# Five products of constants by PE in front of each expert of layer two but the first

## The chip, the cores and the metric

The kernel runs on one core of a Trainium2 chip. Its engines are PE (matrix multiplication, with its weight loads shown apart as PEld), DVE, ACT, POOL and SP; SP only issues transfers here. The metric is the time of the kernel on the device in microseconds; the kernel before was timed three times.

## The reference, cut to what matters

The model has two layers on 256 latent and 256 context tokens of width 1024. Each layer has a mixer (two attentions and a convolution) and then a mixture of experts. The change touches the experts of layer two, where only the 256 latent tokens are left and each goes to two of 16 experts:

```
def grouped_moe(h, router_w, router_bias, w1, w3, w2):
    s = jax.nn.sigmoid((h @ router_w).astype(jnp.float32))
    ...
    _, idx = lax.top_k(jnp.where(in_grp, biased, -jnp.inf), TOP_K)
    ...
    for e in range(N_EXPERTS):
        he = (jax.nn.silu(h @ w1[e]) * (h @ w3[e])) @ w2[e]
        out = out + combine[:, e:e + 1] * he
    return out
```

w1 and w3 of an expert are 1024 x 512 and w2 is 512 x 1024, all fp32, so each of the three is 2 MB, and an expert's weights are 6 MB. After the last layer a normalisation gives the output.

## The kernel before, in words

**Steps.** The rows that go to one expert are gathered and padded to blocks of 32. One block is one step: PE makes the product with w1 and w3 in 64 multiplications of 256 columns (bank 2, "W13" below), ACT makes a sigmoid, DVE multiplies (line 1877) and transposes (line 1881), and PE makes the product with w2 in 32 multiplications (bank 3). PE runs the product with w2 of the step before behind the W13 product of this one, so a step of PE is 96 multiplications; POOL scatters the result rows.

**Experts.** The function `expert` (from line 2318) is the part of one expert. It reads the expert's number of blocks from memory into a register (line 2333), runs the first step, and, if there are more blocks, a loop of further steps (from line 2338). Expert 0 to 3 are written out, 4 to 15 are a loop of four turns over three experts. Before its first multiplication `step` (from line 2294) waits for the previous step's hidden rows (line 643, `hold`), for the transposed rows of this one, and for the landing of w1 and w3.

**Weights.** SP issues the loads in the order w1, w3, w2 of each expert, into three groups of three places of 2 MB (the places are ring, HT and parts of area; once XG). Before each load SP waits until the load before the last one has landed, so about two loads are under way, and until PE has freed the place. The list `free` hands two semaphores to the first two multiplications of the next expert: they free the places of w1 and w3 of the expert before. The place of w2 is freed by the drain at line 2315, behind the first step of the next expert.

**The end.** After the last product with w2 (of expert 15) come its scatter, the sum of the two rows of each token, the last normalisation and the stores.

Of the kernel before, what the change touches and what calls it, by code (L numbers as in the profile page):

```python
# [16 lines left out]
DEPTH = 2  # L17
# [22 lines left out]
CHUNK = 512  # L40
# [314 lines left out]
def hybrid_moe_kernel(nc, A):  # L355
# [4 lines left out]
    with ctx:  # L360
        def sb(name, shape, dt=fp32):
            return ctx.enter_context(nc.sbuf_tensor(name, shape, dt))
# [13 lines left out]
        cst = sb("cst", [P, C_W])  # L376
# [144 lines left out]

        ps = ctx.enter_context(nc.psum_tensor("ps", [P, 8, CHUNK], fp32))

        B_W13, B_W2 = 2, 3


        modD = nc.dram_tensor("mod_rows", [DEPTH, 2, 6 * D], fp32).ap()
# [112 lines left out]
        def hold(e, semaphore, value, passed):  # L640

            e.wait_ge(semaphore, value)
            e.sem_inc(passed, 1)
# [5 lines left out]
        ident = cst[:, C_ID:C_ID + P]  # L649
# [16 lines left out]
        def unit_of_slot(x):  # L666

            return ring[:, x] if x < RING else extra[x - RING].rearrange("p (k n) -> p k n", k=KD)

        def is_spare(l, e, turn, w):  # L670

            return isinstance(turn, int) and (e, w) == (GROUPS, 0)

        def spare_of(l):

            if l == DEPTH - 1:
                return [XG[:, 2:TILES + 2].rearrange("p t d -> p (t d)").rearrange("p (k n) -> p k n", k=KD)]
            return [piece.rearrange("p (k n) -> p k n", k=KD // 2) for piece in (gate.rearrange("p c d -> p (c d)"), area[:, AW - UNIT // 2:AW])]
# [22 lines left out]
        def expert_slots(l, e):  # L701

            return EXPERTS[l][0][e % GROUPS]
# [9 lines left out]
        def landed(l, e, x, turn=0):  # L713

            return 16 * pieces(x) * (expert_uses(l, e, x, turn) + 1)
# [1203 lines left out]
        def _(pe):  # L1919
            t_ = nc.tensor  # L1920

            def mm(out, lhsT, rhs, first, last_):
                return t_.matmul(out, lhsT, rhs, start=first, stop=last_)  # L1923
# [91 lines left out]
            for l in range(DEPTH):  # L2015
# [277 lines left out]
                def step(slots, prev_slot, waits, free=(), first=False, up=None, release=None):  # L2293
                    b = pe.snap(done)
                    if not first:
                        hold(pe, g_rdy[l], b, pe_passed)
                    pe.wait_ge(xt_rdy[l], b + 1)
                    if waits:
                        for q in range(2):
                            pe.wait_ge(ring_full[slots[q]], waits[q])  # L2300
                    half = NG // 2
                    up = up or [[unit_of_slot(x)] for x in slots[:2]]
                    for k in range(KD):
                        lhsT = xT[:, k * SLOT:(k + 1) * SLOT]
                        for j in range(NG):
                            last = mm(ps[SLOT * j:SLOT * (j + 1), B_W13, 0:NW], lhsT,
                                      up[j // half][k * len(up[j // half]) // KD][:, k % (KD // len(up[j // half])), j % half * NW:(j % half + 1) * NW],
                                      k == 0, k == KD - 1)
                            if k * NG + j < len(free):
                                last.then_inc(ring_free[free[k * NG + j]], 1)  # L2310
                    last.then_inc(w13_full[l], 1)
                    if not first:
                        w2_product(b, prev_slot, waits[2] if waits else None)
                        if release is not None:
                            pe.drain().then_inc(ring_free[release], 1)
                    pe.reg_add(done, done, 1)

                def expert(e, turn, at_e, first=False):

                    sl, before = expert_slots(l, e), expert_slots(l, e - 1)  # L2320
                    waits = [landed(l, e, x, turn) for x in sl[:2]]
                    free, release = [], None
                    if not first:
                        waits.append(landed(l, e - 1, before[2], turn))

                        free = [before[0], before[1]]
                        if l == DEPTH - 1 or isinstance(turn, int) and e < GROUPS:
                            release = before[2]
                        elif not isinstance(turn, int):
                            free.append(expert_slots(l, e - 2)[2])  # L2330
                    else:
                        waits.append(None)
                    blocks = pe.value_load(nb[0:1, bass.ds(at_e, 1)], min_val=1, max_val=TOK // SLOT)
                    up = [spare_of(l) if is_spare(l, e, turn, w) else [unit_of_slot(sl[w])] for w in range(2)]
                    if l == 0 and is_spare(l, e, turn, 0):
                        pe.wait_ge(spare_in, 16)
                    step(sl, before[2], waits, free, first, up, release)
                    with pe.If(blocks > 1):

                        hold(pe, ring_full[sl[2]], landed(l, e, sl[2], turn), pe_passed)  # L2340
                        with pe.Fori(1, blocks):
                            step(sl, sl[2], None, up=up)

                expert(0, 0, 0, True)
                for e in range(1, GROUPS + 1):
                    expert(e, 0, e)
                with pe.Fori(1, (E_N - 1) // GROUPS) as i:
                    for q in range(GROUPS):
                        expert(1 + q, i, 3 * i + 1 + q)
# [32 lines left out]
```

## Time and profile before

| | us |
|---|---|
| median of three runs | 1142.3 (1140.0 to 1145.42) |
| the profiled execution, time | 1148.53 |
| the profiled execution, span of the trace | 1146.7 |
| PE busy in the span | 924.9 (81%) |
| DMA into ring from the expert weights, issue to landing, median | 10.2 |
| mean granted clock of PE | 0.9 |

The profile is of one execution. Its time holds 1.83 us that lie around the span. A granted clock of 1.00 is 2.4 GHz, of 0.50 is 1.2 GHz; a value between is a mean over a stretch that has both. PE's busy time counts a multiplication until its modelled end, so neighbours overlap.

### The profile page before, as it was taken

How to read it: one execution, taken by the hardware profiler on the slowest of the kernel's cores; microseconds unless marked ns; L12 is line 12 of the kernel's file. 1: busy time of each engine (PE TensorE's matmuls, PEld its weight loads, DVE VectorE, ACT ScalarE, POOL GpSimd, SP SyncE). 2: the span in 40 equal slices, each digit the busy share in tenths (PEclk: the TensorE clock that was granted, in tenths of full speed). 3: DMA queues.
4: the chain of work that ended last, by engine and by line, in shares of the span. 5: the costliest groups of instructions: out<-in, count | busy, mean ns of one | idle time of the engine just before them, and what ended most of it. 6: DMA issues, size and time to landing. Idle time of an engine off the chain costs nothing. (4 is left out here: it accounts for less than half of the span.)

```text
span 1146.7 us, 23528 instructions
## 1 busy us (share of the span) xinstructions
PE 924.9 (81%) x8592; PEld 545.5 (48%) x8593; DVE 448.7 (39%) x1049; ACT 248.4 (22%) x491; POOL 227.0 (20%) x375
## 2 busy tenths in 40 slices
PE   3999999988897599979779399999896577555871
PEld 3546446455454356646446166544653344322440
DVE  2187515654554323323222566426633322111223
ACT  2100111543321122313122030124421112111110
POOL 4100000110020144425333220001000133211231
PEclk9999999989988699989899699999897689877886
DMA  9998601820004989999999977128206899999993
GB/s 348 380 413 299 245 3 71 339 93 1 1 19 159 374 316 405 422 416 417 422 420 411 388 288 283 74 74 340 110 1 225 323 413 398 417 428 426 417 379 117
DMA packets 54014, 317.45 MB, mean 277 GB/s; under 512 B 7288, under 2 KB 8008, under 8 KB 35136
## 3 DMA queue, kind: packets, MB, share of 16 engines
q1 hardware_dynamic: 41168, 286.21, 62.1%
q0 software_dynamic: 9584, 20.02, 4.9%
q10 hardware_dynamic: 3200, 10.36, 2.4%
q8 instruction: 43, 0.70, 0.2%
q14 instruction: 19, 0.16, 0.0%
HBM read 308.62 MB, written 12.65 MB: 280 GB/s over the span
## 5 line engine op out<-in xcount | busy, mean ns | idle before, releaser
L1923 PE MATMUL ps<-ring,area 128*32 128x256 f32 x3808 | 243.5, 407 | 63.6 <-DMA ring<-in_w 38.5
L1923 PE MATMUL ps<-ring,HT 128*128 128x512 f32 (+1 forms) x576 | 259.1, 603 | 2.3 <-ACT HT L1164 1.5
L1923 PE MATMUL ps<-area 128*32 128x256 f32 (+3 forms) x1928 | 225.3, 399 | 20.9 <-DVE area L1821 9.7
L1923 PEld LDWEIGHTS ps<-ring,area 128*32 128x32 f32 x3808 | 142.1, 117 | 154.3 <-issue 49.8
L1923 PEld LDWEIGHTS ps<-ring,HT 128*128 128x128 f32 x576 | 110.4, 197 | 128.7 <-issue 126.5
L1923 PEld LDWEIGHTS ps<-area 128*32 128x32 f32 (+2 forms) x1928 | 129.7, 139 | 45.4 <-issue 25.3
L1923 PE MATMUL ps<-HT,area 128*32 128x256 f32 x704 | 93.9, 426 | 40.9 <-DMA area<-in_w 32.3
L971 POOL DMA_INDIRECT expert_rows<-area x64 | 69.0, 1079 | 248.9 <-DVE area L1871 111.2
L1844 DVE STREAM_TRANSPOSE area<-area 128x256 f32<-128x256 f32 x65 | 29.0, 446 | 226.0 <-PE ps L1923 225.7
L1217 ACT ACTIVATE area<-ps 128x128 f32<-128x128 f32 x63 | 17.5, 278 | 362.7 <-PE ps L1923 362.7
L961 POOL DMA_INDIRECT area<-h_rows,area x68 | 71.3, 1048 | 100.4 <-DVEq L1834 42.4
L1217 ACT ACT_TABLE_LOAD x63 | 80.8, 1283 | 38.7 <-issue 37.6
L1923 PEld LDWEIGHTS ps<-HT,area 128*32 128x32 f32 x704 | 51.6, 122 | 76.1 <-issue 59.1
L1923 PE MATMUL ps<-HT,ring 128*128 128x256 f32 (+1 forms) x320 | 85.0, 423 | 1.9 <-DVE HT L1403 1.8
L1439 DVE SCALAR_TENSOR_TENSOR area<-area,CW 128x512 f32<-128x512 f32 (+1 forms) x120 | 68.8, 614 | 4.5 <-issue 0.5
L1923 PEld LDWEIGHTS ps<-HT,ring 128*128 128x128 f32 x320 | 60.1, 191 | 21.6 <-issue 15.3
L855 POOL TENSOR_SCALAR ms<-ss 128x1 f32<-128x1 f32 (+1 forms) x22 | 9.4, 428 | 237.1 <-DVE ss L1608 162.6
L1923 PE MATMUL ps<-ring,SC 128*32 128x512 f32 (+1 forms) x576 | 48.2, 489 | 9.3 <-POOLq L992 8.3
L876 POOL DMA_DIRECT2D area<-in_b_ada x20 | 10.2, 515 | 222.7 <-ACTq L637 96.4
L1156 ACT ACTIVATE area<-ps 128x512 f32<-128x512 f32 (+1 forms) x48 | 25.2, 526 | 101.6 <-PE ps L2203 68.0
L1570 DVE TENSOR_REDUCE mx<-ps 128x2 f32<-128x1024 f32 (+1 forms) x36 | 37.6, 1045 | 16.1 <-PE ps L1923 15.8
L1869 DVE COPY area<-ps 128x256 f32 (+1 forms) x39 | 16.6, 425 | 62.6 <-PE ps L1923 59.3
(221 smaller groups left out, 734.5 us busy)
## 6 DMA issues: line engine op xcount, KB each, us to landing
ring<-in_w SPq DMA_DIRECT2D x64, 2048.0 KB, 10.2
ring<-in_w_ada SPq DMA_DIRECT2D x24, 2048.0 KB, 18.7
area<-in_w SPq DMA_DIRECT2D x21, 1024.0 KB, 11.2
ring<-in_w_in SPq DMA_DIRECT2D x10, 2048.0 KB, 16.3
HT<-in_w SPq DMA_DIRECT2D x10, 2048.0 KB
area<-in_w SPq DMA_DIRECT2D x10, 2048.0 KB, 10.5
ring<-in_w_out SPq DMA_DIRECT2D x4, 2048.0 KB, 8.4
area<-expert_rows ACTq DMA_DIRECT2D x12, 512.0 KB, 5.2
```

The source lines that it names most:

```text
L855: link(g.tensor_scalar(m_, s_, 1.0 / n, EPS, ALU.mult, ALU.add))
L876: pool.dma_start(bias_of(n)[32 * j:32 * j + 32, :], A["b_ada"][l_:l_ + 1, col:col + CHUNK].broadcast_to([32, CHUNK])).then_inc(bias_in[n % ...
L961: pool.indirect_dma_start(xg[:, r * NW:(r + 1) * NW], None, h2_rows, bass.IndirectOffsetOnAxis(ap=at_, axis=0), bounds_check=routed(l) * N ...
L971: pool.indirect_dma_start(y_rows, bass.IndirectOffsetOnAxis(ap=sidx[r], axis=0), ym[:, r * NW:(r + 1) * NW], None, bounds_check=2 * routed ...
L1156: taken(s.activation(aT[:, k % 2, 0:kw], bank(key)[:, 0:kw], ACT.Identity), key)
L1217: s.activation(sg, ps[:, B_W13, 0:P], ACT.Silu).then_inc(si_rdy[l], 1)
L1439: v.scalar_tensor_tensor(dst, src, w, dst, ALU.mult, ALU.add)
L1570: v.tensor_reduce(mx[:, b], pair[:, :, 0:kw], AX.X, ALU.max)
L1844: v.transpose(xT, xs).then_inc(xt_rdy[l], 1)
L1869: v.tensor_copy(dst, ps[:, B_W2, 0:NW]).then_inc(y_rdy[l], 1)
L1923: return t_.matmul(out, lhsT, rhs, start=first, stop=last_)
```

## The change

The expert part of layer two gets five multiplications of the identity matrix with the first 512 columns of the constants, into bank 5 of ps, which nothing reads. They stand behind the load of the count and ahead of every wait of the step, in each expert but the first: 15 experts, 75 multiplications. They wait for nothing and set no semaphore.

```diff
-        B_W13, B_W2 = 2, 3
+        B_W13, B_W2, B_IDLE = 2, 3, 5
...
                     blocks = pe.value_load(nb[0:1, bass.ds(at_e, 1)], min_val=1, max_val=TOK // SLOT)
+                    if l == DEPTH - 1 and not first:
+                        for _ in range(5):
+                            mm(ps[:, B_IDLE], ident, cst[:, 0:CHUNK], True, True)
```

First place: PE, layer two, from the end of expert 0's part to the first multiplications of expert 1, before. TENSOR_LOAD is the load of the count; hidden_made, xT_copied and ring_full are the waits for the hidden rows, for the transposed rows and for the landed weights.

```order
L2316 ISA
L2341 COMPARE_AND_BRANCH
L2338 UNCONDITIONAL_BRANCH
L2333 TENSOR_LOAD area
L2333 ISA x2
L2297 REGISTER_ALU [waits hidden_made_1]
L1923 MATMUL ps<-ring,area 32x256 [waits ring_full_3,ring_full_2,xT_copied_1]
L1923 MATMUL ps<-ring,area 32x256 x31
L1923 MATMUL ps<-ring,area 32x256 [waits ring_full_1,y_copied_1,gT_copied_1]
```

The same place now:

```order
L2316 ISA
L2344 COMPARE_AND_BRANCH
L2341 UNCONDITIONAL_BRANCH
L2333 TENSOR_LOAD area
L2333 ISA x2
L1923 MATMUL ps<-cst 128x512 x5
L2297 REGISTER_ALU [waits hidden_made_1]
L1923 MATMUL ps<-ring,area 32x256 [waits ring_full_3,ring_full_2,xT_copied_1]
L1923 MATMUL ps<-ring,area 32x256 x31
L1923 MATMUL ps<-ring,area 32x256 [waits ring_full_1,y_copied_1,gT_copied_1]
```

The five multiplications have come in between the load of the count and the three waits. Everything behind them stands as it did.

Second place: PE, the third expert of the loop's body, which is expert 6, 9, 12 and 15, before:

```order
L2316 ISA
L2341 COMPARE_AND_BRANCH
L2338 UNCONDITIONAL_BRANCH
L2333 ISA
L2333 TENSOR_LOAD area
L2333 ISA x2
L2297 REGISTER_ALU [waits hidden_made_1]
L2300 ISA [waits ring_full_5,xT_copied_1]
L1923 MATMUL ps<-ring,area 32x256 [waits ring_full_0]
L1923 MATMUL ps<-ring,area 32x256 x31
```

And now:

```order
L2316 ISA
L2344 COMPARE_AND_BRANCH
L2341 UNCONDITIONAL_BRANCH
L2333 ISA
L2333 TENSOR_LOAD area
L2333 ISA x2
L1923 MATMUL ps<-cst 128x512 x5
L2297 REGISTER_ALU [waits hidden_made_1]
L2300 ISA [waits ring_full_5,xT_copied_1]
L1923 MATMUL ps<-ring,area 32x256 [waits ring_full_0]
L1923 MATMUL ps<-ring,area 32x256 x31
```

Here too the five stand behind the load and ahead of the waits. The steps inside the `If` (a second and third block) have none in front.

## Rows read from the trace of the kernel before

**Rows 1.** Busy time by engine in stretches of layer two's experts.
```profile
core 0: us, PE busy (x) PEld busy (x) DVE busy (x) ACT busy (x) POOL busy (x), PEclk, DMA share, GB/s
911.00:914.00 3.00, 1.74 (x35) 1.14 (x33) 1.16 (x4) 1.56 (x2) 0.26 (x2) 1.00 0.14 52
914.00:920.00 6.00, 3.86 (x72) 2.51 (x64) 1.59 (x5) 1.56 (x2) 1.80 (x3) 1.00 0.99 362
1000.00:1060.00 60.00, 31.70 (x384) 16.64 (x384) 7.18 (x20) 6.24 (x8) 9.32 (x16) 0.73 1.01 425
1085.00:1112.00 27.00, 21.52 (x384) 13.48 (x384) 8.22 (x23) 6.25 (x8) 11.34 (x18) 0.99 1.01 420
1112.00:1119.00 7.00, 6.55 (x68) 3.12 (x72) 0.00 (x0) 0.00 (x0) 0.12 (x1) 0.55 0.47 198
```

**Rows 2.** SP's own waits, 905 to 925: total us, times, longest.
```profile
SPq L643 <- PE ps L1923: 8.7, 2, 7.9
SPq L643 <- PEq L2315: 4.3, 1, 4.3
```

**Rows 3.** The same, 925 to 1110.
```profile
SPq L643 <- DMA ring<-in_w: 102.2, 23, 5.7
```

**Rows 4.** Timeline of PE: start, length, what, [idle before <- releaser].
```profile
905.15 6.07 PE L1923 MATMUL ps<-ring,area 128*32 128x256 f32 x64 [7.24 <-DVE area L1844]
912.48 5.39 PE L1923 MATMUL ps<-ring,area 128*32 128x256 f32 x96 [1.26 <-DVE area L1877]
922.13 0.64 PE L1923 MATMUL ps<-HT,area 128*32 128x256 f32 x2 [4.27 <-issue]
...
955.45 0.41 PE L1923 MATMUL ps<-HT,area 128*32 128x256 f32 x2 [1.88 <-DMA area<-in_w]
```

**Rows 5.** Timeline of PE, experts six and seven.
```profile
971.94 5.12 PE L1923 MATMUL ps<-ring,area 128*32 128x256 f32 x64 [2.54 <-DMA ring<-in_w]
...
987.79 7.07 PE L1923 MATMUL ps<-ring,area 128*32 128x256 f32 x96 [2.62 <-DMA ring<-in_w]
```

**Rows 6.** Timeline of PE, experts twelve to fifteen.
```profile
1064.56 6.57 PE L1923 MATMUL ps<-ring,area 128*32 128x256 f32 x64 [8.02 <-DMA ring<-in_w]
...
1073.90 10.57 PE L1923 MATMUL ps<-ring,area 128*32 128x256 f32 x192 [1.04 <-issue]
1084.97 5.39 PE L1923 MATMUL ps<-ring,area 128*32 128x256 f32 x96 [0.50 <-issue]
...
1106.56 2.11 PE L1923 MATMUL ps<-area 128*32 128x256 f32 x34
1112.45 6.52 PE L1923 MATMUL ps<-ring,area 128*32 128x256 f32 x64 [3.78 <-DMA ring<-in_w]
1118.80 1.90 PE L1923 MATMUL ps<-area 128*32 128x256 f32 x32
1122.45 1.93 PE L1923 MATMUL ps<-ring,area 128*32 128x256 f32 x32 [1.75 <-DVE area L1881]
```

**Rows 7.** Timeline of SP's DMA issues.
```profile
913.21 0.33 SPq L811 DMA_DIRECT2D ring<-in_w  x1
918.03 0.33 SPq L813 DMA_DIRECT2D ring<-in_w  x1
923.46 5.04 SPq L811 DMA_DIRECT2D ring<-in_w  x2
```

**Rows 8.** Timeline of PE, projections of layer two.
```profile
740.04 13.90 PE L1923 MATMUL ps<-ring,HT 128*128 128x512 f32 x32
```

**Rows 9.** Multiplications into ps: duration in ns, min/median/max, first and last start.
```profile
L1923 PE MATMUL ps<-ring,HT x576: 379/592/1201, 70.2 to 876.5; 128*128 128x512 f32 x181, 128*128 128x256 f32 x11
```

**Rows 10.** Line 2333, the count's load, 917 to 923: ns, start.
```profile
L2333 PEldq TENSOR_LOAD <-area x1: 301/301/301, 921.0 to 921.0; - x1
```

**Rows 11.** The same, 1060 to 1110.
```profile
L2333 PEldq TENSOR_LOAD <-area x3: 297/302/306, 1083.7 to 1107.5; - x3
```

**Rows 12.** Line 2338, the branch behind a step, 917 to 923: ns, start.
```profile
L2338 PEldq COMPARE_BRANCH  x1: 2812/2812/2812, 918.2 to 918.2; - x1
```

## The prediction

> **What bounds the kernel now.** I read the busy table by stretches first. In the experts of layer two the DMA share is 0.99 to 1.01 from 914 to 1112 at 362 to 425 GB/s, while PE is busy 31.70 of 60 us in 1000 to 1060 [rows 1]: the weights set the pace. SP's own waits say the same for 925 to 1110: 102.2 us in 23 waits end with a landing in ring [rows 3], and the view lists no wait for PE in that stretch. Two parts are different, and the change is judged in them.
>
> At the start, 905 to 925, SP waits for PE: 8.7 us in two waits, and 4.3 us for the drain at line 2315 [rows 2]. Between 911 and 914 the DMA share is 0.14 [rows 1], since the load of expert 3 that SP issues at 913.21 [rows 7] needs a place that the first multiplications of expert 1, at 912.48 [rows 4], set free. What comes late here is late for every load behind it.
>
> At the end PE is the bound. Expert 12 starts at 1064.56 when its weights have landed, and then the three loads of the count in 1060 to 1110, from 1083.7 to 1107.5 [rows 11], are those of experts 13, 14 and 15. So expert 12 has three steps: 64 and 32 multiplications from 1064.56, and 192 from 1073.90 that end at 1084.47. From there to 1106.56 + 2.11 = 1108.67 PE never waits for a landing: a 0.50 us gap at 1084.97, and others of about a microsecond between steps. Then it waits 3.78 us, to 1112.45, for w3 of expert 15 [rows 6]. All that follows hangs on that W13 product: the chain goes over it, the w2 product at 1118.80 and the last one at 1122.45 to the end.
>
> **The price of five products.** 32 multiplications of 128x512 by 128x128 weights take 13.90 us with the clock at its upper level, 0.434 each [rows 8], weight loads hidden. Five are 2.17 us. At the lower level I take twice that, 4.34; the longest single record of the form, 1201 ns against a median of 592 [rows 9], agrees with a factor of two. They wait for nothing, so they run at once behind the load of the count, which PE's sequencer reads ahead of the array (1107.5 for expert 15 [rows 11], while the array works until 1108.67). They fill the beginning of a wait and leave its end idle.
>
> Here a rule of the Trainium skill would raise the price: "FP8 and Floating Point Precision", section TensorE Precision Notes, has true fp32 as four passes through the array. By it 512 columns would be 2048 cycles at 2.4 GHz, 0.85 us, and five 4.3. The row does not bear that out: 0.434 us is 1042 cycles, two to a column. By the page the sum would be that of the doubled cost below, about 1151; I go by the row.
>
> **Part one: experts 1 and 2, where DMA waits for PE.** Expert 0's W13 product runs from 905.15 to 911.22, then PE waits 1.26 us for the hidden rows [rows 4]. The products put 2.17 in the place of 1.26: expert 1 starts 0.91 later, SP's issue at 913.21 too, and the gap of the DMA queue widens by that. Queued behind them on PE is the whole of expert 1, so the drain comes 0.91 later and with it the issue at 918.03 [rows 7].
>
> In front of expert 2 PE is idle 4.27 us [rows 4], of which 2.81 are the branch behind expert 1's step [rows 12]; the count's load follows at 921.0 [rows 10]. So the products can only start where W13 starts now, some 922.1 + 0.9 = 923.0. PE has then been idle over 4 us, and a wait of 2.5 or 2.6 us elsewhere has already brought the lower clock: 64 multiplications in 5.12, and 96 in 7.07 against 5.39 [rows 5, 6]. I take the lower level, 4.34: W13 of expert 2 starts at 927.4 instead of 922.13, and the load that SP issues at 923.46, which its first multiplications set free, goes out at about 928.7. That is no loss as long as the load ahead keeps the queue busy. It went out at 918.03 and now at 918.9; SP's next issue after 923.46 comes 4.7 us later, when it has landed (the row holds two issues, 0.33 each, in 5.04 us [rows 7], so the second went out at 928.17). With the shift it has landed by 929.1, and the new load's first bytes come about a microsecond after its issue (the share climbs at 914 after the issue at 913.21 [rows 1, 7]), at 929.7. I add 0.8 for this gap (between 0, if the clock stays up, and 5.3, if nothing of it is hidden). Together the stream of weights is 0.91 + 0.8 = 1.7 us later.
>
> **Part two: experts 3 to 12, beside the DMA.** Experts 3, 4 and 5 add 2.17 each to a PE that had 1.88 us to spare at expert 5 [rows 4]. It falls some 9 us behind the weights, and that matters only if a place is then freed too late. Three groups of places give three experts' lead: the place that expert e frees is for expert e + 2 or later, whose load goes out some 10 us or more later. The tightest is HT for expert 5, freed by expert 3; I find 1 to 2 us to spare there with the delays above and cost it at nothing; with less cover it is the rival below. Experts 6 and 7 waited 2.54 and 2.62 us [rows 5], and from 1000 to 1060 PE is idle for 28.3 of 60 us [rows 1]: PE has caught up soon after expert 7, and what it gains or loses up to expert 12 is cover. Expert 12 starts with the landing, so 1.7 later than now. Its wait, 8.02 less 2.17, is still 5.8 us, so its W13 stays at the lower clock as now (6.57).
>
> **Part three: experts 13, 14 and 15, where PE is the bound.** At expert 13 the products take up the gap of 0.50: 2.17 - 0.4 = 1.8 on the path. At expert 14, where no gap is left, 2.17. At expert 15 2.17. So without the shift the W13 product of expert 15 could start at 1108.67 + 1.8 + 2.17 + 2.17 = 1114.8, against 1112.45 now: 6.1 us of products, 3.78 of them in the wait, 2.4 on the path. In return PE has no wait left and the clock does not fall. Now 64 multiplications take 6.52 [rows 6], and 96 at the upper clock 5.39, so 64 are 3.59: 2.9 less. The product ends at 1118.4 instead of 1119.0, that is 0.5 earlier. The load of w3 also lands 1.7 later, at 1114.1 in place of 1112.45, as PE does, and PE remains the later one.
>
> **The sum.** +1.7 from part one, +2.4 and -2.9 from part three: +1.2 us. The profiled execution's 1148.53 would become 1149.7. It was 6.2 above the median of 1142.3, so I put the same difference on the median: 1143.5 us. The runs differ by 5.4 us among themselves, and a measurement of this kernel can tell about 0.5%, 5.7 us, from no change: what I forecast is no change.
>
> **Rivals.** *The clock stays up everywhere.* If the products in the waits also keep the upper clock through expert 12's wait, its W13 gives 6.57 - 3.59 = 3.0 back. PE could then start expert 15 at 1114.8 + 1.7 - 3.0 = 1113.5, and the landing at 1114.1 becomes the bound: W13 ends at 1117.7, 1.3 earlier than now, and the time is 1141.0. For it: PE's gaps shrink in 15 places, and at 955.45 a wait of 1.88 did not bring the lower clock [rows 4]. Against: the products stand at the start of the wait and 5.8 us stay empty. The Trainium skill has this as a rule ("TensorE: Matmul & The Clock Gate", section Why this matters for your kernels: no long idle gaps between bursts if the clock is to stay up); rows 5 agree as to short gaps, and by the rule this rival is right only where the rest of the gap is short.
>
> *Late places stop the weights.* This one ends slower. If nothing hides the 5.3 us of expert 2's products and expert 3's 2.17 also hold the load into HT, the stream is 0.9 + 5.3 + 2.2 = 8.4 later, and with -0.5 at the end it is +7.9: 1150.2. It decides once SP's issue of expert 4's first load is more than about 5 us later than now while the DMA share in the 5 us behind it drops under 0.9. For it: SP did wait for PE here [rows 2]. Against: two loads are under way, and each is about 5 us of transfer.
>
> *The products cost as much as at the lower clock everywhere.* Then 4.34 instead of 2.17 falls on experts 13 to 15, 6.5 more, and 1 to 2 more at the start: 1151 or so. Only a clock that does not rise, or a weight load that is not hidden, could do it; the stretch 1085 to 1112 has a clock of 0.99 [rows 1].
>
> *The products do nothing.* Were they absent from the trace, the time would be 1142.3. The order of PE's instructions has them in six places, three written out and three in a loop of four turns.
>
> **Chances.** The forecast 0.60, the clock rival 0.17, late places 0.12, the doubled cost 0.05, the rest 0.06 for things not seen here, of either sign. Slower by over 0.5% (over 1148.0) takes the late places, the doubled cost and a little of the rest: 0.14. Faster by over 0.5% (under 1136.6) is in none of the cases worked out; I leave 0.06. Within 0.5%: 0.80. The range is from 1138.5, the clock rival less half the spread of the runs, to 1150, just short of late places in full.
>
> **What would show it.** In the profile after: 75 multiplications from the constants of 128x512, a group of five in some 2.2 us; those of expert 2 in about 4.3 us. SP's issue at 913.2 about 0.9 later, expert 12's start 1 to 3 us later. The W13 product of expert 15 with no wait for a landing in front and in some 3.6 us, its start 2 to 4 us later. PEclk 1.00 between 1085 and the end of that product. It is wrong if expert 12 starts over 4 us later (part one or two), if expert 12's W13 takes under 5 us (the clock rival), or if five products take over 3 us in experts 13 to 15.

## The result, and the profile after

| | before | after |
|---|---|---|
| median of the timed runs, us | 1143.37 (1140.0 to 1145.42, 5 runs) | 1154.38 (1151.09 to 1158.46, 5 runs) |
| the profiled execution, time and span | 1148.53, 1146.7 | 1151.09, 1149.3 |
| mean granted clock of PE | 0.900 | 0.933 |
| MATMUL records in the trace | 8592 | 8742 |

The ratio of the runs is 1.0078, with a 95% interval of 1.0054 to 1.0103: the change costs 8.9 us (6.2 to 11.8). I had forecast +1.2, no change that can be told.

The profiled execution of before, 1148.53, took longer than each of its five timed ones, that of after is the shortest of its five. What differs between them ahead of the change is seen in one number: expert 0's first product starts at 905.15 before and at 898.93 after. So I compare from that start on. It leaves 1146.7 - 905.15 = 241.6 us before and 1149.3 - 898.93 = 250.4 after, +8.8, which is what the timed runs say. All times "after expert 0's start" below are made in this way. One trace is one execution; how far such numbers differ from one execution to the next is measured at the end of the experiments.

The first thing to see is the count. 75 products were added in the code, and 8742 - 8592 = 150 records. This is the view by tile for the constants, PE, in the experts of layer two; the columns are count, duration in ns (min/median/max), first and last start:

```profile
L1923 PE MATMUL ps<-cst x150: 592/592/1061, 904.7 to 1117.6; 128*128 128x512 f32 x150
```

The timeline of PE after (start, length, what, idle before and who ended it), which answers to [rows 4 to 6]:

```profile
898.93 5.80 PE L1923 MATMUL ps<-ring,area 128*32 128x256 f32 x64 [7.60 <-DVE area L1844]
...
909.14 5.39 PE L1923 MATMUL ps<-ring,area 128*32 128x256 f32 x96
916.60 6.25 PE L1923 MATMUL ps<-cst 128*128 128x512 f32 x10 [2.07 <-issue]
```

```profile
1049.20 0.41 PE L1923 MATMUL ps<-HT,area 128*32 128x256 f32 x2 [3.92 <-DMA area<-in_w]
...
1057.56 4.55 PE L1923 MATMUL ps<-cst 128*128 128x512 f32 x10 [1.29 <-issue]
1064.27 3.66 PE L1923 MATMUL ps<-ring,area 128*32 128x256 f32 x64 [2.16 <-DMA ring<-in_w]
...
1081.15 4.56 PE L1923 MATMUL ps<-cst 128*128 128x512 f32 x10
1085.64 5.39 PE L1923 MATMUL ps<-ring,area 128*32 128x256 f32 x96
...
1113.61 4.56 PE L1923 MATMUL ps<-cst 128*128 128x512 f32 x10
1118.10 3.66 PE L1923 MATMUL ps<-ring,area 128*32 128x256 f32 x64
```

Each group of five products is ten records and holds PE for 4.49 us (1081.15 to 1085.64, start to start), not the 2.17 of the forecast. From expert 0 on PE waits for no landing until expert 11, at 1049.20; before, the first such wait was that of expert 5, at 955.45 [rows 4]. Behind expert 12 there is no wait at all: the W13 product of expert 15 starts when its products end and runs at the upper clock, 3.66 us. It starts 1118.10 - 898.93 = 219.2 us after expert 0, against 207.3 before.

SP's issues after, to set beside [rows 7], and its waits for PE in 898 to 925 and in 925 to 1110 [rows 2, 3]:

```profile
909.91 0.33 SPq L811 DMA_DIRECT2D ring<-in_w  x1
...
923.69 2.57 SPq L811 DMA_DIRECT2D ring<-in_w  x2
...
939.85 0.33 SPq L811 DMA_DIRECT2D HT<-in_w  x1
```

The issue into HT before, which [rows 7] does not show:

```profile
938.60 0.33 SPq L811 DMA_DIRECT2D HT<-in_w  x1
```

The waits after:

```profile
SPq L643 <- PE ps L1923: 15.6, 2, 10.8
```

```profile
SPq L643 <- DMA ring<-in_w: 102.1, 23, 6.1
...
SPq L643 <- PE ps L1923: 3.4, 2, 1.8
```

Its waits for PE have grown from 8.7 to 15.6 us, and in the second stretch there are now two, 3.4 us, where the view had none. After expert 0's start, the first issue, the one behind expert 2's products and the one into HT come at 11.0, 24.8 and 40.9 us, against 8.1, 18.3 and 33.4.

The stretches that answer to [rows 1] (the same columns):

```profile
905.00:909.00 4.00, 4.00 (x10) 1.52 (x8) 1.07 (x4) 1.36 (x2) 1.41 (x3) 1.00 0.08 27
...
1000.00:1060.00 60.00, 49.13 (x527) 25.15 (x527) 8.98 (x25) 7.80 (x10) 13.59 (x22) 0.97 1.01 424
...
1112.00:1119.00 7.00, 7.00 (x61) 3.17 (x56) 1.79 (x5) 1.56 (x2) 2.03 (x4) 1.00 0.49 200
```

In 905 to 909 the queue stands nearly empty (0.08) while PE makes products; from 1000 to 1060 PE is busy 49 of 60 us instead of 31.7 at the same DMA share; in 1112 to 1119 the clock is 1.00, where it was 0.55.

### The profile page after: what moved, and what is told of

The parts are those of the page before. It is cut to its first block and busy times, and to the rows that moved or that the text cites. A ratio compares the mean times of both kernels' runs of the same rounds, so it can differ in the third digit from the quotient of the medians.

```text
span 1149.3 us, 23828 instructions
## 1 busy us (share of the span) xinstructions
PE 965.3 (84%) x8742; PEld 558.4 (49%) x8743; DVE 448.9 (39%) x1049; ACT 248.3 (22%) x491; POOL 226.4 (20%) x375
## 5 line engine op out<-in xcount | busy, mean ns | idle before, releaser
L1923 PE MATMUL ps<-ring,HT 128*128 128x512 f32 (+1 forms) x576 | 255.8, 597 | 2.5 <-ACT HT L1164 1.2
L1923 PE MATMUL ps<-ring,area 128*32 128x256 f32 x3808 | 228.8, 389 | 32.2 <-DVE area L1844 13.1
L1923 PE MATMUL ps<-area 128*32 128x256 f32 (+3 forms) x1928 | 216.4, 389 | 19.4 <-DVE area L1821 9.7
L1923 PEld LDWEIGHTS ps<-ring,area 128*32 128x32 f32 x3808 | 134.1, 113 | 119.0 <-issue 27.8
L1923 PEld LDWEIGHTS ps<-area 128*32 128x32 f32 (+2 forms) x1928 | 126.5, 135 | 42.5 <-issue 23.3
L1923 PE MATMUL ps<-HT,area 128*32 128x256 f32 x704 | 87.8, 406 | 23.2 <-DMA area<-in_w 18.9
L1923 PE MATMUL ps<-cst 128*128 128x512 f32 (+1 forms) x182 | 75.7, 560 | 11.6 <-issue 11.6
L1923 PEld LDWEIGHTS ps<-HT,area 128*32 128x32 f32 x704 | 48.7, 117 | 57.6 <-issue 37.0
L1923 PEld LDWEIGHTS ps<-cst 128*128 128x128 f32 x182 | 32.0, 193 | 54.1 <-issue 54.1
L855 POOL TENSOR_SCALAR ms<-ss 128x1 f32<-128x1 f32 (+1 forms) x22 | 9.4, 426 | 230.6 <-DVE ss L1608 159.4
```

What stands on the lines that cost most here:

```text
L855: link(g.tensor_scalar(m_, s_, 1.0 / n, EPS, ALU.mult, ALU.add))
```

## The experiments

The theory after the first result, T: a product of fp32 is two records, five of 512 columns are 4.5 us, and they cost where PE is on the path. That is in two places: the first experts, where they hold back SP's loads, and experts 13 to 15. The rival, R: the products disturb transfers or code fetch, so that the cost goes with the amount of added work wherever it stands. All kernels are the changed one with these lines edited; each was timed on one chip with the kernel before, except where the text says that there is one trace alone.

**Half the columns.**

```diff
-                            mm(ps[:, B_IDLE], ident, cst[:, 0:CHUNK], True, True)
+                            mm(ps[:, B_IDLE, 0:CHUNK // 2], ident, cst[:, 0:CHUNK // 2], True, True)
```

> Five products in front of the same 15 experts, but of 256 columns instead of 512. Theory (each product is two MATMUL records of 0.45 us at 512 columns, so five are 4.5 us, and they cost where PE is on the path: experts 1 and 2, then 13 to 15): five are now 2.2 us, the size that the prediction had assumed, and its own working should hold: stream of weights +1.7 us, products on the path at the end +2.4, clock -2.9, so +1.2 us, within 0 to +4. Rival (products disturb the weight transfers or PE's instruction fetch, so the cost goes with the amount of added work, wherever it stands): half of the change's +8.9, +4.5 us.

Ratio 1.0009 (0.9988 to 1.0030): +1.0 us (-1.4 to +3.4). R's +4.5 (half of +8.9) is outside. From expert 0's start to the end it is 1145.2 - 903.43 = 241.8 us, +0.2. PE's timeline:

```profile
909.56 2.42 PE L1923 MATMUL ps<-cst 128*128 128x256 f32 x10
911.92 5.39 PE L1923 MATMUL ps<-ring,area 128*32 128x256 f32 x96
```

```profile
1064.23 6.01 PE L1923 MATMUL ps<-ring,area 128*32 128x256 f32 x64 [4.93 <-DMA ring<-in_w]
...
1111.69 2.43 PE L1923 MATMUL ps<-cst 128*128 128x256 f32 x10
1114.05 3.66 PE L1923 MATMUL ps<-ring,area 128*32 128x256 f32 x64
```

A group is 2.36 us from start to start (909.56 to 911.92), the size that I had given to five full products, and with it the sum of the prediction, +1.2, comes out. Expert 12 starts at 160.8 us, and expert 15's product, with no wait before it, ends at 1114.05 + 3.66 - 903.43 = 214.3 us, against 213.8 before. So the weights are 1.4 us later at expert 12, and the stretch from there to the end of expert 15's product is 53.5 us for 54.4, 0.9 shorter; the forecast had +1.7 and -0.5.

**The first three alone.**

```diff
-                    if l == DEPTH - 1 and not first:
+                    if l == DEPTH - 1 and not first and isinstance(turn, int):
```

> Five products of 512 columns in front of experts 1, 2 and 3 alone. Theory: these are the ones that hold SP's loads; the weights come 5 to 6.5 us later for all of the layer, and the end is as in the kernel before, with its wait of 3.8 us and its lower clock: +5 to +6.5 us. Expert 12's first product starts about 165 us after expert 0's instead of 159.4. Rival (cost by amount of work, 3 of 15 places): +1.8 us.

Ratio 1.0032 (1.0012 to 1.0053): +3.7 us (1.4 to 6.1). Less than I expected in the middle, and its interval holds both; the trace tells more:

```profile
903.02 6.17 PE L1923 MATMUL ps<-ring,area 128*32 128x256 f32 x64 [7.23 <-DVE area L1844]
...
913.61 5.39 PE L1923 MATMUL ps<-ring,area 128*32 128x256 f32 x96
920.41 4.55 PE L1923 MATMUL ps<-cst 128*128 128x512 f32 x10 [1.41 <-issue]
```

```profile
1065.43 5.19 PE L1923 MATMUL ps<-ring,area 128*32 128x256 f32 x64 [7.35 <-DMA ring<-in_w]
...
1113.88 6.55 PE L1923 MATMUL ps<-ring,area 128*32 128x256 f32 x64 [4.11 <-DMA ring<-in_w]
```

Expert 1 is 10.6 us after expert 0 instead of 7.3, expert 12 is 162.4 instead of 159.4, and the end is as before: a wait of 4.11 and a W13 product of 6.55. Expected were about 165, and the 3 us that are missing come up again at the end of the experiments. From expert 0's start to the end: 244.9, +3.3. Expert 2's products, at the upper clock here (4.55), took 6.25 in the changed kernel's trace.

**The loop alone**, experts 4 to 15.

```diff
-                    if l == DEPTH - 1 and not first:
+                    if l == DEPTH - 1 and not isinstance(turn, int):
```

> Five products of 512 columns in front of experts 4 to 15 alone. Theory: the weights keep their times (expert 12 starts 159 to 160 us after expert 0); the end gets 3 x 4.5 us of products, less 0.4 and less the wait of 3.8, less 2.9 for expert 15's product at the upper clock, less another 2.9 if expert 12's is at the upper clock too: +3.5 us with it, +6.4 without. Rival (amount of work, 12 of 15 places): +7.1 us, with the weights later too.

Ratio 1.0057 (1.0035 to 1.0079): +6.5 us (4.0 to 9.0). With the row above it gives 3.7 + 6.5 = 10.2, against 8.9 for all places. T's +6.4 and R's +7.1 both lie in the interval, so the time alone does not tell them apart here.

```profile
1061.31 3.66 PE L1923 MATMUL ps<-ring,area 128*32 128x256 f32 x64 [1.95 <-DMA ring<-in_w]
...
1110.67 4.56 PE L1923 MATMUL ps<-cst 128*128 128x512 f32 x10
1115.16 3.66 PE L1923 MATMUL ps<-ring,area 128*32 128x256 f32 x64
```

From expert 12's start to the end of expert 15's first product: 1115.16 + 3.66 - 1061.31 = 57.5 us, against 1112.45 + 6.52 - 1064.56 = 54.4 before: +3.1, with expert 12's product at the upper clock (3.66). But expert 12 itself started at 162.2 us, 2.8 late, though SP never waited for PE there, as R would have it. One more trace of this kernel was taken:

> Five fp32 products in front of experts 4 to 15 alone, one more look. In the first look expert 12 started at 162.2 us after expert 0, 2.8 later than in both looks at the kernel before, though SP never waited for PE. If products beside the transfers slow these, it is 161.5 to 163 again; if it was chance, 159 to 160.

```profile
1061.34 6.15 PE L1923 MATMUL ps<-ring,area 128*32 128x256 f32 x64 [4.51 <-DMA ring<-in_w]
...
1117.73 3.66 PE L1923 MATMUL ps<-ring,area 128*32 128x256 f32 x64
```

Expert 12 starts 1061.34 - 901.33 = 160.0 us after expert 0, so most of the 2.8 us was chance. This time its product runs at the lower clock (6.15), so from its start to the end of expert 15's it is 60.1 us, +5.7. The two traces come to nearly the same end, 247.2 and 247.5 us after expert 0's start, +5.6 and +5.9.

**Expert 1 alone, and expert 2 alone.**

```diff
-                    if l == DEPTH - 1 and not first:
+                    if l == DEPTH - 1 and isinstance(turn, int) and e == 1:
```

> Five products of 512 columns in front of expert 1 alone. Theory: 4.5 us of products in the place of the wait of 1.26, so expert 1 and SP's next two issues are 2.9 to 3.3 us later (in the trace 11.0 us after expert 0's start instead of 8.1), the issue after them 3 us later at most, and the time is +3 us. The end is as in the kernel before. Rival (cost by amount of work): +0.6 us.

Ratio 1.0027 (1.0006 to 1.0047): +3.1 us (0.7 to 5.4). The first of SP's issues comes at 914.07 - 902.68 = 11.4 us, expert 12 at 162.9.

> Five products of 512 columns in front of expert 2 alone. Theory: the two issues that hang on expert 1 keep their times (8.1 and 12.9 us after expert 0's start); the one that expert 2's first multiplications free is later by the products less the time that PE had been idle there anyway, 2 to 6 us by the clock, of which about 4 us are covered by the load under way: 0 to +3 us on the time. Rival (amount of work): +0.6 us.

(the same line with `e == 2`). Ratio 1.0029 (1.0014 to 1.0044): +3.3 us (1.6 to 5.0).

```profile
905.59 5.39 PE L1923 MATMUL ps<-ring,area 128*32 128x256 f32 x96 [1.26 <-DVE area L1877]
914.27 7.61 PE L1923 MATMUL ps<-cst 128*128 128x512 f32 x10 [3.29 <-issue]
```

```profile
906.33 0.33 SPq L811 DMA_DIRECT2D ring<-in_w  x1
911.15 0.33 SPq L813 DMA_DIRECT2D ring<-in_w  x1
922.72 1.02 SPq L811 DMA_DIRECT2D ring<-in_w  x2
```

And the stretch ahead of the last issues (the columns of [rows 1]):

```profile
919.50:923.00 3.50, 3.50 (x29) 1.51 (x31) 0.00 (x0) 0.00 (x0) 0.00 (x0) 0.87 0.02 9
```

The issues that hang on expert 1 keep their times (8.2 and 13.1 us); the one behind expert 2's products comes at 922.72 - 898.10 = 24.6 instead of 18.3. After 3.29 us of idle time the products take 7.61, most of it at the lower clock. The load under way covers only the first 2 to 3 us of the 6.3 us of delay: from 919.50 to 923.00 the DMA share is 0.02. The issue into HT is 5.3 us late in this trace (38.8), expert 12 starts at 164.1, 4.7 late, and the timed runs say +3.3. The rival's +0.6 is outside both intervals, for expert 1 only just. The two do not add up to the first three's +3.7: behind expert 1's products, expert 2's come after a gap of 1.4 us at the upper clock.

**Is it the passes of fp32?**

```diff
-                            mm(ps[:, B_IDLE], ident, cst[:, 0:CHUNK], True, True)
+                            mm(ps[:, B_IDLE], cst[:, 0:P // 2].bitcast(mybir.dt.bfloat16), cst[:, 0:CHUNK // 2].bitcast(mybir.dt.bfloat16), True, True)
```

> The same five products of 512 columns in all 15 places, but the constants are read as bf16. Theory (an fp32 product is two MATMUL records of two cycles a column each, a bf16 one is a single record of one cycle a column): 75 records, 0.22 us each, five in 1.1 us. They fit the wait of 1.26 in front of expert 1 and three times 1.1 fit the wait of 3.8 in front of expert 15; what is left of it is under 1.5 us, so expert 15's first product runs at the upper clock: -2.9 us against the kernel before, or 0 if the clock falls. Rival (each product costs the same whatever it reads, by its count): as the change, +8.9 us.

Ratio 0.9984 (0.9966 to 1.0002): -1.8 us (-3.9 to +0.2). The same 75 products, and the +8.9 are gone. A product that reads bf16 also reads half the bytes; this run alone does not separate that from the number of passes. Its records:

```profile
L1923 PE MATMUL ps<-cst x60: 376/379/634, 909.9 to 1113.6; 128*128 128x512 bf16 x60
```

```profile
1112.95 1.03 PE L1923 MATMUL ps<-cst 128*128 128x512 bf16 x4 [0.16 <-issue]
1115.52 3.66 PE L1923 MATMUL ps<-ring,area 128*32 128x256 f32 x64 [1.55 <-DMA ring<-in_w]
```

60 records for 75 products, where fp32 had 150. Each group shows four, many of them behind 0.16 us of idle time that no releaser explains, so I take the first of each to be missing from the trace; then one product is one record. They start 0.22 us apart (1.03 for four, the last 0.38 long). From the end of expert 14's product to the start of the last wait it is 1.2 us: a quarter of the 4.5. And the wait of 1.55 that is left does not bring the lower clock: 3.66.

**A version that might beat both.** If nothing but the wait in front of expert 15 is filled, its product gets 2.9 us shorter for nothing. Three kernels have products in front of experts 6, 9, 12 and 15 alone: four of fp32, eight of bf16, twelve of bf16.

```diff
-                    if l == DEPTH - 1 and not first:
-                        for _ in range(5):
+                    if l == DEPTH - 1 and not isinstance(turn, int) and e == GROUPS:
+                        for _ in range(4):
```

> Four products of 512 columns (3.5 us) in front of experts 6, 9, 12 and 15 alone. Theory: those of expert 15 fit the wait of 3.8 us in front of it, so nothing on the path gets longer, and its first product runs at the upper clock in 3.6 instead of 6.5 us: -2.9 us, so 0.2 to 0.3% faster than the kernel before. Expert 12's stays at the lower clock or not, without effect, since the landing in front of expert 14 holds PE within 0.1 us of its old time. Rival (amount of work): 16 of 75 products, +1.9 us.

> Eight bf16 products of 512 columns (1.7 us) in front of experts 6, 9, 12 and 15 alone, so none at the start of layer two and none in front of experts 13 and 14. Theory: expert 15's wait of some 3.8 us is cut to about 2, its first product runs at the upper clock in 3.7 instead of 6.5 us, nothing else moves: -2.8 us. Rival (what is left of the wait still brings the lower clock, as the waits of 2.5 did in front of experts 6 and 7 before): 0.

> Twelve bf16 products of 512 columns (2.6 us) in front of experts 6, 9, 12 and 15 alone. With eight of them expert 15 still waited 2.36 us and its first product took 5.35; where 1.55 us were left it took 3.66. Theory (the clock falls by the length of what is left idle): some 1.5 us are left, the first product takes 3.7 us, and from expert 0's start to the end it is 241.4 less 2.4 to 2.8 us: -2.5 us, ratio 0.9978. Rival (a gain that the trace shows but a later wait takes back): ratio 1.000.

```profile
1056.95 3.66 PE L1923 MATMUL ps<-ring,area 128*32 128x256 f32 x64 [3.25 <-DMA ring<-in_w]
...
1089.25 0.41 PE L1923 MATMUL ps<-HT,area 128*32 128x256 f32 x2 [2.78 <-DMA area<-in_w]
...
1102.74 3.70 PE L1923 MATMUL ps<-cst 128*128 128x512 f32 x8
1106.37 3.66 PE L1923 MATMUL ps<-ring,area 128*32 128x256 f32 x64
```

```profile
1100.84 1.90 PE L1923 MATMUL ps<-cst 128*128 128x512 bf16 x8
1105.09 5.35 PE L1923 MATMUL ps<-ring,area 128*32 128x256 f32 x64 [2.36 <-DMA ring<-in_w]
```

```profile
1100.03 2.76 PE L1923 MATMUL ps<-cst 128*128 128x512 bf16 x12
1103.65 3.66 PE L1923 MATMUL ps<-ring,area 128*32 128x256 f32 x64 [0.85 <-DMA ring<-in_w]
```

Ratios: four fp32 1.0002 (0.9984 to 1.0020), eight bf16 0.9984 (0.9964 to 1.0004), twelve bf16 0.9994 (0.9975 to 1.0014). In the traces expert 15's product has no wait and takes 3.66, then a wait of 2.36 and 5.35 (with eight bf16 products the rival's case, not the 3.7 that I expected), then 0.85 and 3.66. From expert 0's start to the end it is 239.4, 241.5 and 237.8 us, against 241.6 and 241.4 in two traces of the kernel before. But the traced executions of the first and third were the shortest of their twelve (1139.32 and 1136.59, where the medians are 1143.91 and 1144.01), and none of the three is shown faster: the first's interval excludes the -2.9 that I expected, the third's just holds its -2.5, the second's -1.8 is not clear of zero. R's +1.9 for the first lies in its interval too. In the first, expert 12's products kept the clock up, PE came early to the landing for expert 14, waited 2.78 us there and fell to the lower clock (5.13 us from the start of that W13 product to the next one, 1089.25 to 1094.38), and expert 15's products then ran past the landing of its weights. A version that beats both kernels is not shown.

**How far single traces differ.**

> The kernel before without an edit, one more look: how far one execution's stream of weights differs from another's. Expert 12's start after expert 0's was 159.4 us; if single looks scatter by no more than 1 us, the 3 to 6 us of the kernels with products at the start are theirs, and if by 3 us, single looks cannot size them and the timed rounds must. Expected 158 to 163.

```profile
1062.30 6.20 PE L1923 MATMUL ps<-ring,area 128*32 128x256 f32 x64 [8.42 <-DMA ring<-in_w]
...
1110.31 6.09 PE L1923 MATMUL ps<-ring,area 128*32 128x256 f32 x64 [4.33 <-DMA ring<-in_w]
```

Expert 12 starts 1062.30 - 902.83 = 159.5 us after expert 0 (159.4 in the first trace), and the end is 241.4 us (241.6). The two differ by 0.2 us from expert 0's start on, though their times up to it differ by 2.3. Other pairs are not so close: the loop-only kernel has 162.2 and 160.0, and the kernel with bf16 products in all places has expert 12 at 1067.63 - 903.58 = 164.1 us, 4.6 late, where its timed runs are not slower at all.

> The change itself without an edit, again. Theory: +7 to +11 us; 45.5 us of five-product groups at 4.5 us, no wait for a landing in front of expert 15, expert 15's first product at 3.66 us, expert 12's start 163 to 166 us after expert 0's, and from expert 12's start to expert 15's 53 to 54 us against 47.9.

```profile
1066.29 5.21 PE L1923 MATMUL ps<-ring,area 128*32 128x256 f32 x64 [4.19 <-DMA ring<-in_w]
...
1121.75 3.66 PE L1923 MATMUL ps<-ring,area 128*32 128x256 f32 x64
```

The change again: ratio 1.0102 (1.0062 to 1.0142), +11.7 us (7.1 to 16.2), which agrees with the first within the intervals. From expert 0's start to the end it is 1152.8 - 900.79 = 252.0 us, +10.6. The "45.5 us" in the expectation is a slip of mine; 15 groups at 4.5 are 67 us. Expert 12 starts 165.5 us after expert 0 (165.3 in the first trace). From there to expert 15's start it is 55.5, a little over the 53 to 54 expected, as expert 12's product ran partly at the lower clock (5.21).

Where the delay of the weights arises can be read by cutting the stretch at the issue into HT. It comes at 33.4 and 34.1 us before, at 40.9 and 38.9 with the change and at 38.9 with the first three places alone: 5 to 7 us late, in all three traces, ahead of the loop. From this issue to expert 12's start it is 123.5 to 128.0 us in the fourteen traces: 126.0 and 125.4 before, 123.5, 125.1 and 125.3 with fp32 products at the start alone, 124.4, 126.6, 127.7 and 125.8 with five fp32 products in the loop, 128.0 with bf16. So the first three places alone make the whole delay up to HT; that their expert 12 came at 162.4 and not at 165 is within this scatter. Whether products beside the transfers slow these by a microsecond, a weak form of R, is not decided by it.

## Why the prediction was wrong, step by step

**The price of five products: the step that failed.** I had written "32 multiplications of 128x512 by 128x128 weights take 13.90 us with the clock at its upper level, 0.434 each" and "Five are 2.17 us". The row is right, but it counts records, and a product of fp32 in the code is two of them. Five cost 4.49. What would have told me was on record: the order of the instructions has 32 products for W13 (1 + 31), the code makes 16 for w2, and the timeline has 64 and 32 for them. I even wrote "64 multiplications" for the 32 of the code, in the description of the kernel too.

The Trainium skill had the right number ("FP8 and Floating Point Precision", section TensorE Precision Notes: true fp32 is four passes). Two records of two cycles a column are four. The estimate from the skill's figure for five, 4.3 us, is what the trace bears out with 4.49. I set the skill's figure against the row, found two cycles a column, and threw the figure out. The case that I had priced at 1151, a doubled cost, is the one that came true (1151 is 8.7 over the 1142.3 of before, and +8.9 and +11.7 were measured); I gave it 5%, and for a wrong reason (the clock). All three of my signs of being wrong came: five products over 3 us (4.49), expert 12 over 4 us later (5.9 and 6.0), and its W13 product under 5 us (3.66, in the first trace).

**Part one, +1.7: measured +6.0** (expert 12's start 159.4 and 159.5 before, 165.3 and 165.5 after). The mechanism was right: the first issue waits for expert 1's multiplications and goes 2.9 us later, which is 4.49 less the wait of 1.26 and a little, not 0.9. The load behind expert 2 goes 6.5 later (24.8 for 18.3), and the one into HT 939.85 - 898.93 = 40.9 us after expert 0's start for 33.4. A second error is smaller: I had let the load under way cover all but 0.8 us of expert 2's delay. In the kernel with expert 2 alone it covered 2 to 3 of 6.3 us, and the queue stood empty for about 4. What I had called the tightest place, HT behind expert 3, and costed at nothing, is one more wait of SP for PE now (1.8 us, the longest of the two in 925 to 1110); how much of the 6.0 it carries was not taken apart.

**Part two, nothing: not refuted.** The traces of the loop alone have expert 12 at 162.2 and 160.0, 2.8 and 0.6 later than before, with nine groups beside the transfers ahead of it, and from 925 on SP waited for PE in neither. The path to it was not as I had it: PE did not catch up behind expert 7 but, with groups of twice the length, only at expert 11.

**Part three, -0.5: measured +3.1 and +5.0** (expert 12's start to the end of expert 15's first product: 57.5 for 54.4 in the first traces, 59.1 for 54.1 in the second ones). With the right price my own terms give it: 3 x 4.49 - 0.4 - 3.78 = 9.3 on the path, -2.9 for expert 15's clock, +6.4; where expert 12's product also keeps the upper clock, another -2.9, +3.5. The clock term itself, 6.52 to 3.6, was right: 3.66.

**The clock rival** was half right: as the groups are longer, only 2.16 us of expert 12's wait were left, and its product ran at 3.66 in the first trace. In the second, with 4.19 left, it took 5.21. It does not help, since PE is then on the path with more products than that saves.

**Late places**, priced at +7.9, happened in part. Its own test was an issue more than 5 us late and a DMA share under 0.9 in the 5 us behind it. In the first trace it is 6.5 us late and the share from 923.69 to 928.69 is 0.86; in the second it is 4.4 late and the share 0.94. Over 925 to 1112 the share was 1.00 in the first.

**The price that halves.** With 256 columns the group has the length that I had assumed, and the sum +1.2 met +1.0 (-1.4 to +3.4). That is the strongest sign that the price was the main error; the interval is too wide to judge the small terms of the paths.

**The chances do not add up as written.** "Slower by over 0.5%" got 0.14, but the late places and the doubled cost that it takes in are 0.12 + 0.05 = 0.17 alone.

## What to carry to other kernels

Before a row prices an operation, match its count with the code's: how many records does one call leave? Here one line of the instruction order beside one of the timeline would have done it. When the Trainium skill and a row differ by about two, look for the unit before choosing. Filler work at the head of a wait is free only where its engine has more slack than its length, and the engine that bounds nothing on average can bound the first and the last microseconds of a stage.

## What the runs showed of the hardware

The branch behind expert 1's step [rows 12] got shorter when fp32 products stood in front of expert 1, and with it the gap before expert 2: 4.27 us before, 2.07 after, 1.41 with the first three alone. This is line 2341 of these kernels (the branch that was 2338), in PE's sequencer, in the changed kernel and in the one with the first three:

```profile
L2341 PEldq COMPARE_BRANCH  x1: 1098/1098/1098, 914.8 to 914.8; - x1
```

```profile
L2341 PEldq COMPARE_BRANCH  x1: 438/438/438, 919.3 to 919.3; - x1
```

2.81 us before, 1.10 and 0.44 here. It holds in all fourteen traces: with fp32 products in front of expert 1 this branch took 0.43 to 1.10 us (five traces), without them, or with the short bf16 ones, 2.30 to 4.08 (nine). A guess is that the sequencer gets ahead while the array makes products; what it does in that time was not tested.

The length of a W13 product goes with the wait in front of it, but not by the length of the wait alone. At experts 6 to 15, in all kernels, waits up to 2.2 us were followed by 3.66 (0.85, 1.55, 1.95 and 2.16 are in the rows above), or by 5.39 where the row is a whole step of 96, and 3.78 and more by 4.9 to 6.6. Between them both happened: 2.36 by 5.35, 2.54 by 5.12 and 3.01 (expert 6 of the bf16 kernel) by 5.35, but 3.25, in the kernel with four fp32 products, by 3.66, and 3.52, at expert 11 of the change's second trace, by 3.45 from its start to the next product, as at the upper clock. Elsewhere a shorter gap was enough: in the change's first trace ten records took 6.25 behind 2.07 us of idle time in front of expert 2, where 4.55 is their length at the upper clock. So a wait need not be filled to the end to keep the upper clock, and how much may be left differs from one place to the next.
